# FFN inputs scaled by the root before the product, from the seventh pair of column tiles on

## The reference, cut to what matters

```
D_FF_2 = 2816
def rms_norm(x, g):
    y = x * rsqrt(mean(x * x, axis=-1) + EPS)
    return y * g
def causal_dwconv(x, w):            # width 3, along the tokens, each channel for itself
def conv_ffn(h, w_up, w_conv, w_down):
    gate, up = split(causal_dwconv(h @ w_up, w_conv), 2)
    return (silu(gate) * up) @ w_down
...
    ffn = conv_ffn(rms_norm(x, g_pre_ffn[i]), w_ffn_up[i], w_ffn_conv[i], w_ffn_down[i])
    x = x + rms_norm(ffn, g_post_ffn[i])
```

## Time and profile before

| | |
|---|---|
| median of 3 runs | 1244.31 us (1242.66 to 1246.69) |
| the profiled execution | 1246.46 us, its span 1244.7 us |
| mean granted TensorE clock | 0.993 |
| busy PE / DVE / ACT | 98% / 72% / 59% |
| FFN 0, up and down projection | about 664 to 854 us of the span |
| FFN 1, the same | about 1013 to 1202 us |

### The profile page before, as it was taken

How to read it: one execution, slowest core, us unless ns; L and a number is a source line. 1 busy time by engine, 2 the same in 40 slices (tenths; PEclk the granted TensorE clock), 3 DMA queues, 4 the chain that set the end, 5 groups by cost and what they waited for, 6 DMA issues and landing times.

```text
span 1244.7 us, 24316 instructions
## 1 busy us (share of the span) xinstructions
PE 1216.5 (98%) x10110; PEld 1191.1 (96%) x10110; DVE 899.4 (72%) x1544; ACT 738.6 (59%) x1258; POOL 18.6 (1%) x36
## 2 busy tenths in 40 slices
PE   9999999999999999999999999999999999999997
PEld 8999799999999999999999999999889899999996
DVE  6986566764447876445876999956887778999656
ACT  6873456664445765434655666655767766665655
POOL 1120000000000000000000000000000000000000
PEclk9999999999999999999999999999899999999998
DMA  7233154555552665664763666473374246665640
GB/s 280 83 122 100 40 170 159 197 183 183 170 166 94 221 195 198 189 197 123 232 193 124 196 195 202 145 247 114 122 255 152 73 136 189 202 189 177 224 136 34
DMA packets 59753, 205.51 MB, mean 165 GB/s; under 512 B 6739, under 2 KB 9340, under 8 KB 59516
## 3 DMA queue, kind: packets, MB, share of 16 engines
q1 hardware_dynamic: 57536, 201.21, 50.0%
q10 hardware_dynamic: 2108, 2.75, 0.7%
HBM read 202.87 MB, written 1.06 MB: 164 GB/s over the span
## 4 chain that ended last, share of the span: by engine, by line
PE 82%; DVE 9%; ACT 6%; issue 2%; DMA 1%; ACTq 0%; DVEq 0%
PE PS L378 67%; PE PS L423 6%; DVE WL L363 2%; PE PS L390 2%; ACT WH L356 1%; DMA RAW<-wpack 1%; PE PS L472 1%; PE PS L2470 1%; PE PS L530 1%; ACT EE L2628 1%; DVE X L1925 1%; DVE UL L550 1%; ACT L542 1%; DMA X<-xin 1%; PE PS L707 0%
## 5 line engine op out<-in xcount | busy, mean ns | idle before, releaser
L363 DVE TENSOR_TENSOR WL<-RAW,WH 128x1024 fp32r<-128x1024 f32 (+2 forms) x387 | 461.3, 1197 | 204.4 <-ACT WH L356 203.8
L356 ACT ACTIVATE WH<-RAW 128x1024 fp32r<-128x1024 f32 (+2 forms) x387 | 392.3, 1034 | 203.6 <-PE PS L378 169.8
L378 PE MATMUL PS<-UH,WH 128*128 128x256 f32 (+1 forms) x1464 | 414.7, 283 | 6.1 <-DVE WL L363 3.9
L378 PE MATMUL PS<-UH,WL 128*128 128x256 f32 (+1 forms) x1464 | 411.4, 281 | 0.0
L378 PE MATMUL PS<-UL,WH 128*128 128x256 f32 (+1 forms) x1464 | 411.3, 281 | 0.0
L378 PEld LDWEIGHTS PS<-UH,WH 128*128 128x128 f32 x1464 | 275.9, 188 | 7.4 <-issue 3.6
L378 PEld LDWEIGHTS PS<-UL,WH 128*128 128x128 f32 x1464 | 276.4, 189 | 0.0
L378 PEld LDWEIGHTS PS<-UH,WL 128*128 128x128 f32 x1464 | 274.6, 188 | 0.0
L378 PE MATMUL PS<-HH,WH 128*128 128x272 f32 (+1 forms) x512 | 144.8, 283 | 0.0
L378 PE MATMUL PS<-HH,WL 128*128 128x272 f32 (+1 forms) x512 | 144.7, 283 | 0.0
L378 PE MATMUL PS<-HL,WH 128*128 128x272 f32 (+1 forms) x512 | 144.3, 282 | 0.0
(11 more groups left out here) (414 smaller groups left out, 2069.9 us busy)
## 6 DMA issues: line engine op xcount, KB each, us to landing
RAW<-wpack SPq DMA_DIRECT2D x361, 512.0 KB, 4.2
RAW<-wpack SPq DMA_DIRECT2D x18, 384.0 KB, 3.5
RAW<-wpack SPq DMA_DIRECT2D x6, 256.0 KB, 2.7
C<-cst SPq DMA_DIRECT2D x1, 1072.0 KB, 5.8
HB<-bias_rows ACTq DMA_DIRECT2D x1, 1024.0 KB, 6.4
out<-X SPq DMA_DIRECT2D x4, 256.0 KB, 2.3
X<-xin SPq DMA_DIRECT2D x2, 272.0 KB, 5.6
X<-xin ACTq DMA_DIRECT2D x2, 272.0 KB, 5.6
```

Of the source, the lines that this page charges most:

```text
L356: a.e.activation(WH[n % NH][:, 0:w], RAW[n % NR][:, 0:w], ACT.Copy).then_inc(*a.mark("wh", n))
L363: v.e.tensor_tensor(WL[n % NH][:, 0:w], RAW[n % NR][:, 0:w], WH[n % NH][:, 0:w].bitcast(f32), ALU.subtract).then_inc(*v.mark("wl", n))
L378: ins = t.e.matmul(o, part(n, hw, kw, a, b), x(kx), start=first and not i and not p, stop=last and i == len(kcs) - 1 and p == 2)
```

## The change

From pair U0 = 6 on, the input of the up projection is X x root x gain, and no root is multiplied in behind the product.

- DVE multiplies X by the root, two blocks at a time, into M, in its iterations 0 to 3 behind the FZs (event "xr"). ACT makes the high parts VXH of M x gain at the end of its iterations 0 to 3 (it waits for "xr"), DVE the low parts VXL in its iterations 1 to 4, behind the FZs.
- PE's pairs from 6 on take VXH and VXL as moving operands and wait, block by block, for the low part.
- The FZ instructions of pairs 6 to 21 are gone. ACT's y and DVE's taps read the PSUM bank directly; ACT waits for PE's product. The bank is free again when the second tap has read it.
- In front of the very first matmul of pair 6 stands one more matmul with the same weights and the same input cut to 128 columns. Its result is overwritten by the next.
- VXL0 (blocks 0 to 3) lies where TMA is, VXL1 and VXL2 (4 and 5, 6 and 7) where SQ0 and SQ1 are; VXH has a place behind FZ.

```diff
-        def products(t, o, n, kcs, a, b, xh, xl, ready, first=True, last=True):
+        def products(t, o, n, kcs, a, b, xh, xl, ready, first=True, last=True, short=0):
...
+                if short and not i:
+                    t.e.matmul(o[:, 0:short], part(n, 1, kw, a, b), xh(kx)[:, 0:short], start=True, stop=True)
...
+        U0 = 6
+        def vxl(j):
+            return VXL[0][:, j, :] if j < 4 else VXL[j // 2 - 1][:, j % 2, :]
+
+        def ffn_value(layer, u, m):
+            return PS[:, banks.at["ffn", layer, u, m], 0:S] if u >= U0 else FZ[layer][(2 * u + m) % 4][:, :]
...
+                elif u >= U0:
+                    for m in range(2):
+                        b = banks.take(t, ("ffn", layer, u, m), ("tap", layer, u, m, 2))
+                        products(t, PS[:, b, 0:S], n + m, pairs, 0, 128, lambda k: VXH[layer][:, k, :], vxl,
+                                 lambda k: ("ul", f"fx{layer}", k), short=128 if (u, m) == (U0, 0) else 0).then_inc(
+                                     *t.mark("ffn", layer, u, m))
...
-                    a.wait_ge("fz", layer, u, m)
+                    a.wait_ge("ffn" if u >= U0 else "fz", layer, u, m)
...
-                    a.e.activation(y[:, :], FZ[layer][(2 * u + m) % 4][:, :], ACT.Copy,
+                    a.e.activation(y[:, :], ffn_value(layer, u, m), ACT.Copy,
...
+                if u < 4:
+                    a.wait_ge("xr", layer, u)
+                    for j in (2 * u, 2 * u + 1):
+                        split_hi(a, (f"fx{layer}", j), VXH[layer][:, j, :], M[:, j, :], g(f"gpf{layer}", j))
...
+                    if u >= U0:
+                        continue
                     v.wait_ge("ffn", layer, u, m)
...
+                if 0 < u < 5:
+                    for j in (2 * u - 2, 2 * u - 1):
+                        split_lo(v, (f"fx{layer}", j), vxl(j), M[:, j, :], g(f"gpf{layer}", j), VXH[layer][:, j, :])
+                if u < 4:
+                    v.e.tensor_tensor(M[:, 2 * u:2 * u + 2, :], X[:, 2 * u:2 * u + 2, NM:T], both(RR[0][:, 0:S]),
+                                      ALU.mult).then_inc(*v.mark("xr", layer, u))
...
-                    taps(v, y, FZ[layer][(2 * p + m) % 4], name, 3 * (f + 22 * half),
+                    taps(v, y, ffn_value(layer, p, m), name, 3 * (f + 22 * half),
```

More of the change, by code:

```diff
@@ L307, in program @@
         ONE = ONER[:, :].bitcast(f32)
-        SQ = [sb(f"SQ{i}", [128, 2, T]) for i in range(2)]
+        SQ, VXL = [], []
+        for i in range(2):
+            sc = ExitStack()
+            if i == 0:
+                sb("PADQ", [128, 32], scope=sc)
+            VXL.append(sb(f"VXL{i + 1}", [128, 2, S], f32r, scope=sc))
+            sc.close()
+            SQ.append(sb(f"SQ{i}", [128, 2, T]))
         ACC = [sb(f"ACC{i}", [128, 2, T]) for i in range(2)]
         RR = [sb(f"RR{i}", [128, T]) for i in range(2)]
+        sc = ExitStack()
+        VXL.insert(0, sb("VXL0", [128, 4, S], f32r, scope=sc))
+        sc.close()
         TMA = sb("TMA", [128, 4, T])
@@ L2082, in vector_conv @@
             vector_output(v, "sco")
-        FH, FL, GB, YB, FZ = [], [], [], [], []
+        FH, FL, GB, YB, FZ, VXH = [], [], [], [], [], []
         for layer in range(2):
@@ L2093, in program @@
             FZ.append([sb(f"FZ{layer}{i}", [128, S], scope=sc) for i in range(4)])
+            VXH.append(sb(f"VXH{layer}", [128, 8, S], f32r, scope=sc))
             sc.close()
```

## The result

The changed kernel took 1255.55 us (median, 1252.96 to 1261.1), the kernel before 1243.49 us in the same comparison (1241.56 to 1246.69). The ratio is 1.0088 with a 95% interval of 1.0066 to 1.0111: slower by 8 to 14 us. The profiled execution of after took 1252.96 us with a span of 1251.1, that of before 1246.46 with 1244.7.

The account below looks back on a forecast made before the run. PE, busy 98%, bounds the kernel by its step and its standstills. Each layer: + 7.5 (wait) + 1.7 (low clock) - 5.75 (cadence) = + 3.45 us, both + 6.9, from 1244.31 to 1251.2 us; range 1239 to 1263.

Parts of the forecast that it names:

- the wait: Pair 6's first product: PE waits for DVE's VXL at k = 6, 7.5 us late per layer, some 6.2 us idle.
- the low clock: Behind pair 6's wait the clock falls to 0.50, costing 1.7 us per layer.
- the cadence: From pair 6 through the down projection, 1278 matmuls go from 118.0 to 113.3 ns, saving 5.75 us per layer.
- the 0.8 us at product 7: VXH 0 and 1 stand before WH 7 on ACT, so PE's wait for WL 7 grows by 0.8 us.
- no wait for a bank would come: Pairs 6 and up: product 12's bank is free at about 727, product 20 wants it at about 730.
- my 1.7: Low-clock cost per layer, taken from 3.6 us of dense work at the low level in before.
- the bounds, 0 and 3.2: Low-clock cost per wait: nothing if the level holds, 3.2 us if all 6.83 us lies under work.
- the cadence is slow after a wait for WL at the start of a product: In before, both FFNs went on at the slow step after such a wait, taken as 118.0 ns.
- a product stopped in its middle goes on fast: Pair 6's wait is of this form, so 113.3 ns follows; eight such cases in before went on fast.
- Rival A: The fast cadence does not come behind pair 6: one layer slow 1257.0 us, both 1262.7; chance 0.22.
- DVE's relief worthless: FZs removed in pairs 6 to 21 shorten DVE's pair by 0.67 us, but PE does not wait for DVE there.
- Rival C: The new places of VXH and VXL bring a step under the fast one, at best 0.1065 us, 1233.3 us; chance 0.13.

Follow-up runs that it names:

- Number 3: Changed kernel with U0 = 10 in place of 6, the short 128-column matmul moved along: 1248.07 us beside 1246.01 for before, ratio 1.0018.
- Number 7: Changed kernel with U0 = 22: VXH and VXL made but unused, all FZs kept; 1257.75 us beside 1245.05 for before, ratio 1.0107.
- the filled wait: Changed kernel with 48 matmuls of ones in front of the wait for VXL 6, run twice: ratios to before 1.0119 and 1.0090.
- number 1: Changed kernel without the extra 128-column matmul, all else kept: 1255.39 us beside 1246.01 for before, ratio 1.0069.
- number 2: Kernel before with only the extra 128-column matmul added in front of pair 6: 1246.14 us beside 1246.01, ratio 0.9992.
- 5: Changed kernel with 48 matmuls of ones in front of the wait for VXL 6, first run: 1257.7 us beside 1245.05 for before, ratio 1.0119.
- number 8: Kernel before, unchanged, run once more for a second trace: 1242.47 us, one execution.
- number 9: Kernel before with a pause: PE waits in the middle of product 8 for a tap; 1245.19 us beside 1245.05, ratio 1.0001.
- 11: Kernel before with another order of units in the down projection, blocks needing the last FL later: 1243.97 us beside 1243.96, ratio 0.9992.
- 12: Kernel before with down-projection blocks needing the last FL later, plus a pause in the middle of product 8: 1246.22 us beside 1243.96, ratio 1.0014.
- number 6: Changed kernel with 48 matmuls of ones in front of the wait for VXL 6, second run: 1255.99 us beside 1243.96 for before, ratio 1.0090.
- numbers 10: Changed kernel, unaltered, run once more for a second trace: 1255.66 us beside 1243.96 for before, ratio 1.0077.
- number 4: Changed kernel with U0 = 10 and without the extra 128-column matmul: 1247.43 us beside 1246.01 for before, ratio 0.9997.

## Why the prediction was right, and where its steps were off

The forecast was 1251.2 us, + 6.9 or 0.6%; the measured ratio says + 8 to + 14. The direction, the wait and the low clock held; the size was short, and one term, the cadence, was not what it was taken for.

**The wait.** I put PE's restart at 710.2, DVE's iteration 1 at 685.86 and its iteration 4's VXL 6 at 710.1. The trace has 710.00, 685.87 and 709.46 + 0.40 = 709.86. PE's last start before it is 703.90; it stood idle 5.8 us where I had some 6.2, and began its k = 6 block 7.3 us later than before (702.7), where I had 7.5. Number 3 shows the place by itself: with pair 10 in pair 6's stead the wait is gone and the ratio falls from 1.0088 to 1.0018. Number 7 shows that the added work is not free: where nothing pays it back, it costs as much by itself as the whole change (ratio 1.0107), at the down projection too (5.4 and 2.2 us of waits for FL) and not only the 0.8 us at product 7. That no wait for a bank would come with U0 = 6 held too.

**The low clock.** It fell in both FFNs, as chosen. I had 1.7 us for each; 5.2 us under work at 0.213 and not 0.113 are 5.2 x (1 - 0.113/0.213) = 2.4 us, and the filled wait gave 2.4 and 1.8 us back in its trace. In number 1's trace the same 6.8 us had 3.1 under work, 1.5 us. So my 1.7 was a fair middle, but the term differs from one execution to the next, and the bounds, 0 and 3.2, held it. The page "TensorE: Matmul & The Clock Gate" of the Trainium skill (Why this matters for your kernels) warned of this, and the trace agrees: PE idle for 5.8 us, then 0.50.

**The cadence, the term that failed.** With both terms above, the first traces differ by 4.1 us for each FFN where I had 3.45, so against the execution that I read the sum was nearly right. But I took the slow cadence of before and the fast one behind the wait as facts of the two programs. They are facts of single executions. FFN lengths from the traces:

| | slow | fast |
|---|---|---|
| before | 188.9, 188.8 | 187.0, 187.1 |
| after | 198.7 | 193.0, 192.9, 192.6 |

(Number 1's two FFNs, fast as well, took 191.9 and 191.8.) The forecast is 193 - 188.9, the cheapest of the four pairs. Fast against fast it is 6, slow against slow 9.8. The first traces were this cheap pair, 8.2 us for both layers (and the rest of the span was 1.8 us shorter in after), so their executions are 6.5 us apart where the medians are 12. An estimate of the average from all traces: behind the wait at product 7, the kernels that have before's program up to there (before, numbers 2, 8, 9, 11 and 12) were fast in 7 of 12 FFNs; behind the wait for VXL 6, the changed ones (after, numbers 1, 5, 6 and 10) were fast in 8 of 10. With the table's lengths that is some 187.8 us for an FFN of before and 194.0 for one of after, 12.4 us for both layers. It fits the 12 measured, though from few traces.

Two steps carried this. First, that the cadence is slow after a wait for WL at the start of a product rested on one execution; the second one was fast in both FFNs. Second, that a product stopped in its middle goes on fast, eight times out of eight by the prediction's count in the trace of before, was refuted by numbers 10 and 12, and number 6 was slow behind its filled wait. Rival A, which I gave 0.22, was right in part of the executions; what it lacked was that before isn't always slow.

**What the cadence is worth.** I called DVE's relief worthless, since in the trace of before PE didn't wait for it. That holds at the slow cadence alone. At the fast one before gives over 4 of its 6 us back at the down projection, and the change, whose DVE is lighter by 0.67 us a pair, keeps all of it (198.7 against 192.6). That is what the change could gain, and less than its wait costs. The prediction had it as a gain of 5.75 us over before; over a before that is fast it is some 4 us, what the fast before loses at its down projection.

**Rival C** (a step under the fast one for the new places of the inputs) fell: 355 matmuls in 40 us with VXH and VXL, 113.3 ns like UH and UL. The 109.2 ns that the Trainium skill gives ("TensorE: Matmul & The Clock Gate", Back-to-back issue gap) is its figure for a matmul by itself and not for a stream with weight loads; it was seen in no long stretch of these traces.

**Left open.** What decides which cadence an execution falls into after a wait. How often either kernel is fast is known from few traces. What makes the rest of the span differ by 3.5 us stays open too. Numbers 3 and 4 stay level with before, and their fast FFNs, 187.6 to 187.8 us, are no shorter than before's fast ones; how their executions divide was not seen.

## What to carry to other kernels

When a change moves work ahead of the place that needs it, write down where each engine stands at that moment: PE was three pairs ahead of DVE here, so the seventh pair was too early by 6 us, and the eleventh was late enough. A rate read from one trace of a stretch may belong to that execution; look at a second trace before it becomes a term of the sum. And a faster engine is worth only what the one behind it can follow: the same 4.5 ns a matmul gave 1.8 us in before and 6 in the changed kernel.

## What the runs showed of the hardware that was not expected

A stream of 128x128 weight loads and 256-column fp32r matmuls at full clock runs at 113.3 or 117.8 ns a matmul, for up to 1416 matmuls on end in these traces, across weight buffers and from VXH and VXL to FH and FL. One matmul of 128 columns slipped into the stream without a wait was seen eight times: it turned fast to slow four times out of four (numbers 2, 3 twice, 5), and slow to fast two times out of four (numbers 2 and 5; not in after and not in number 6). After a wait of PE either can follow, from one execution to the next of the same program.

The clock fell to 0.50 behind the unfilled gaps of 6.1 us in all six FFNs seen, behind 2.7 us (number 8), 2.3 us (number 2, FFN 1) and 2.1 us (number 3, both FFNs), but not behind the 2.4 us of number 9 or the 2.1 us of number 4. The length of the gap alone doesn't decide it. With the 6.1 us gaps, 2.9 to 5.6 of the low 6.8 us lay under work.
